# Nine of the sixteen small means of squares of a layer in rounded halves

## The reference, cut to what matters

```python
def rms_norm(x, g):
    xf = x.astype(jnp.float32)
    y = xf * lax.rsqrt(jnp.mean(xf * xf, axis=-1, keepdims=True) + EPS)
    return (y * g.astype(jnp.float32)).astype(x.dtype)
...
def diff_attention(q, k, v, cos, sin, q_g, k_g, lam, lam_init, out_g):
    q = rms_norm(q.reshape(b, s, DA_HEADS, 2, DA_HEAD_DIM), q_g)   # 4 heads, halves of 64
    k = rms_norm(k.reshape(b, s, DA_HEADS, 2, DA_HEAD_DIM), k_g)
    ...  # rotary, two softmaxes, (softmax1 - lam * softmax2) V
    o = rms_norm(o, out_g) * (1.0 - lam_init)
...
def hgrn2_bidirectional(q, z_fwd, z_bwd, inp, gate, lb_fwd, lb_bwd, out_g):
    ...  # gated linear recurrence, forward and backward, 4 heads
    o = rms_norm(o, out_g) * jax.nn.silu(g)
...
for l in range(2):
    proj = rms_norm(x, mix_norm_g[l]) @ w_in[l]                    # 512 x 1024 @ 1024 x 4096
    y_a, y_b = diff_attention(...), hgrn2_bidirectional(...)
    x = x + concat(y_a, y_b) @ w_out[l]
    x = x + conv_glu_ffn(rms_norm(x, ffn_norm_g[l]), ...)          # width 2816
```

## Time and profile before

| | |
|---|---|
| median of 3 runs | 1406.78 us (1406.6 to 1406.83) |
| the profiled execution | 1406.73 us, its span 1404.9 us |
| TensorE busy | 1385.8 us, 99% |
| VectorE busy | 848.9 us, 60% |
| GpSimd busy | 707.9 us, 50% |
| ScalarE busy | 615.2 us, 44% |
| granted TensorE clock | 1.0 throughout |

### The profile page before, as it was taken

One profiled execution on the slowest core, in us unless ns is written; L12 is line 12 of the kernel. 1 busy time (PEld: TensorE's weight loads), 2 busy tenths in 40 slices (PEclk: granted clock), 3 DMA queues, 4 the chain that ended last, 5 costly groups with the idle time before them and its releaser, 6 DMA issues.

```text
span 1404.9 us, 18804 instructions
## 1 busy us (share of the span) xinstructions
PE 1385.8 (99%) x6562; PEld 1118.2 (80%) x6562; DVE 848.9 (60%) x1096; ACT 615.2 (44%) x881; POOL 707.9 (50%) x539
## 2 busy tenths in 40 slices
PE   9999999999999999999998999999999999999999
PEld 6887777877788888888877877778777888888887
DVE  7686797555777676600358758875557766775001
ACT  6352565474444444312444336654744444443111
POOL 2785475337444444444567845652474444444443
PEclk9999999999999999999999999999999999999999
DMA  5222112123233323333222321221122322333333
GB/s 185 76 82 92 46 53 76 46 69 97 80 100 93 103 90 90 105 95 103 90 90 61 90 84 46 71 60 58 61 90 90 105 90 90 99 97 104 90 96 114
DMA packets 37124, 121.31 MB, mean 86 GB/s; under 512 B 4928, under 2 KB 5440, under 8 KB 37056
## 3 DMA queue, kind: packets, MB, share of 16 engines
q1 hardware_dynamic: 36768, 119.84, 27.6%
q10 hardware_dynamic: 288, 0.52, 0.1%
HBM read 114.05 MB, written 2.10 MB: 83 GB/s over the span
## 4 chain that ended last, share of the span: by engine, by line
PE 80%; POOL 6%; issue 6%; DVE 4%; ACT 3%; DMA 0%; POOLq 0%; DVEq 0%; ACTq 0%
PE bank L546 23%; PE bank L548 22%; PE bank L547 22%; PE bank L629 3%; POOL wL L486 2%; PE bank L687 2%; PE bank L705 2%; PE bank L588 2%; POOL rstd L400 1%; POOL wL L480 1%; POOL KK L513 1%; PE bank L696 1%; DVE hL L388 1%; PE bank L660 1%; ACT wH L870 1%
## 5 line engine op out<-in xcount | busy, mean ns | idle before, releaser
L486 POOL TENSOR_TENSOR wL<-raw,wH 128x1024 fp32r<-128x1024 f32 x142 | 342.4, 2411 | 417.5 <-ACT wH L878 356.4
L546 PE MATMUL bank<-hH,wH 128*128 128x512 f32 x1216 | 486.1, 400 | 8.5 <-POOL wL L486 3.5
L548 PE MATMUL bank<-hL,wH 128*128 128x512 f32 x1216 | 474.6, 390 | 0.0
L547 PE MATMUL bank<-hH,wL 128*128 128x512 f32 x1216 | 474.0, 390 | 0.0
L480 POOL TENSOR_TENSOR wL<-raw,wH 128x256 fp32r<-128x256 f32 x268 | 246.8, 951 | 185.0 <-ACT wH L870 185.0
L546 PEld LDWEIGHTS bank<-hH,wH 128*128 128x128 f32 x1216 | 228.3, 188 | 80.5 <-issue 19.2
L548 PEld LDWEIGHTS bank<-hL,wH 128*128 128x128 f32 x1216 | 228.2, 188 | 49.5
L547 PEld LDWEIGHTS bank<-hH,wL 128*128 128x128 f32 x1216 | 228.6, 188 | 44.3 <-issue 0.5
L878 ACT ACTIVATE wH<-raw 128x1024 fp32r<-128x1024 f32 x116 | 122.6, 1057 | 181.1 <-PE bank L548 181.1
L870 ACT ACTIVATE wH<-raw 128x1024 fp32r<-128x1024 f32 x93 | 98.3, 1057 | 141.2 <-PE bank L548 141.0
L546 PE MATMUL bank<-gH,wH 128*128 (+1 forms) x352 | 137.3, 390 | 0.0
(11 more groups left out here) (166 smaller groups left out, 1742.7 us busy)
## 6 DMA issues: line engine op xcount, KB each, us to landing
raw<-wts SPq DMA_DIRECT2D x210, 512.0 KB, 3.5
x<-xT SPq DMA_DIRECT2D x8, 256.0 KB, 5.2
swp<-K SPq DMA_DIRECT2D x32, 64.0 KB, 2.0
swp<-QO SPq DMA_DIRECT2D x32, 64.0 KB, 2.5
outT<-x SPq DMA_DIRECT2D x8, 256.0 KB, 2.0
raw<-wts ACTq DMA_DIRECT2D x2, 256.0 KB, 4.4
raw<-wts SPq DMA_DIRECT2D x2, 256.0 KB, 5.4
W<-pos SPq DMA_DIRECT2D x1, 256.0 KB, 5.8
```

The source lines that it names most:

```text
L486: pool.tensor_tensor(wL[:, s, :], raw[:, s, :], wH[:, s, :].bitcast(F32), ALU.subtract)\
L546: pe.matmul(out, wH[:, s, a:a + P], rhs_h, start=first, stop=False)
L547: pe.matmul(out, wL[:, s, a:a + P], rhs_h, start=False, stop=False)
L548: return pe.matmul(out, wH[:, s, a:a + P], rhs_l, start=False, stop=last)
```

## The change

`PARTED` names nine of the sixteen means: those of slots 13, 14, 18, 25, 26, 27, 30, 31 and 32. For these ScalarE squares the tile twice, once rounded to fp32r into `sqR[:, 0]` and once in fp32 into `sq[:, 1]`. VectorE subtracts the first from the second into `sqR[:, 1]` (`square_low`). TensorE multiplies both fp32r tiles by an fp32r copy of the constants, `meanR`, into the same bank. `sqR` takes the memory of `sq`, so the upper plane is no more free for alternating: all means use plane 1, and each square waits for the mean before it. `meanR` is written once, by ScalarE in slot 12 of the first layer, after the sine.

```diff
+PARTED = [job for s, job in STATS.items() if s < 19 or 24 < s < 33]
...
-        sq = sb("sq", [P, 2, S])
+        sq = sb("sq", [P, 2, S], F32, parts)
+        parts.close()
+        sqR = sb("sqR", [P, 2, S], F32R)
...
+        meanR = sb("meanR", [P, 2 * P], F32R)
...
                     def stat(job):
-                        pe.wait_ge(*squared.at(l, JOB[job] + 1))
+                        if job not in PARTED:
+                            pe.wait_ge(*squared.at(l, JOB[job] + 1))
+                            bank6(("stat", job))
+                            pe.matmul(bank[6][:], cst_at(C_MEAN_H if job in ROPES else C_MEAN_D), sq[:, 1, :],
+                                      start=True, stop=True).then_inc(bank6_full.sem, 1)
+                            return
+                        if l == 0 and JOB[job] == 0:
+                            pe.wait_ge(mean_set, 1)
+                        pe.wait_ge(*part_low.at(l, PARTED.index(job) + 1))
                         bank6(("stat", job))
-                        pe.matmul(bank[6][:], cst_at(C_MEAN_H if job[0] in ("dk", "dq") else C_MEAN_D), sq[:, JOB[job] % 2, :],
-                                  start=True, stop=True).then_inc(bank6_full.sem, 1)
+                        means = meanR[:, P:2 * P] if job in ROPES else meanR[:, 0:P]
+                        pe.matmul(bank[6][:], means, sqR[:, 0, :], start=True, stop=False)
+                        pe.matmul(bank[6][:], means, sqR[:, 1, :], start=False, stop=True).then_inc(bank6_full.sem, 1)
...
                         kind, hd = job
-                        src = sq[:, JOB[job] % 2, :]
+                        j = JOB[job]
+                        if j:
+                            act.wait_ge(*bank6_full.at(l, BANK6[("stat", JOBS[j - 1])] + 1))
...
-                        act.activation(src, of, ACT.Square).then_inc(squared.sem, 1)
+                        if job in PARTED:
+                            act.activation(sqR[:, 0, :], of, ACT.Square)
+                        act.activation(sq[:, 1, :], of, ACT.Square).then_inc(squared.sem, 1)
...
+                                act.activation(meanR[:], cst_at(C_MEAN_D, 2 * P), ACT.Copy).then_inc(mean_set, 1)
...
+                    def square_low(job):
+
+                        dve.wait_ge(*squared.at(l, JOB[job] + 1))
+                        dve.tensor_tensor(sqR[:, 1, :], sq[:, 1, :], sqR[:, 0, :].bitcast(F32), ALU.subtract).then_inc(part_low.sem, 1)
...
                             if lv == CARRY:
                                 states(pair, 0)
+                        if STATS.get(s) in PARTED:
+                            square_low(STATS[s])
                         if step_of(s) is not None:
                             row_max(step_of(s))
```

More of the change, by code:

```diff
@@ L62 @@
          31: ("hgo", 2), 32: ("hgo", 3), 34: ("dao", 3)}
+PARTED = [job for s, job in STATS.items() if s < 19 or 24 < s < 33]
 JOB = {job: j for j, job in enumerate(STATS.values())}
+JOBS = list(JOB)
 OUT_HEADS = [("dao", 0), ("dao", 1), ("dao", 2), ("hgo", 0), ("hgo", 1), ("hgo", 2), ("hgo", 3), ("dao", 3)]
@@ L167, in build @@
     heads = ExitStack()
+    parts = ExitStack()
     ffn = ExitStack()
@@ L265, in build @@
         squared = signal("squared", 16)
+        part_low = signal("part_low", len(PARTED))
+        mean_set = sem("mean_set")
         rstd_ln = signal("rstd_ln", 16)
```

## The result

The changed kernel takes 1412.47 us (median of 6 runs, 1411.71 to 1413.21); before takes 1406.8 beside it (6 runs, 1406.6 to 1407.74). The ratio is 1.0037, with an interval of 1.0026 to 1.0048: slower by 5.7 us between the medians (5.2 by the ratio), and outside the range that was forecast (1404.0 to 1411.9). The profiled execution took 1411.71 us with a span of 1409.9, 4.98 more than the one of before.

What follows compares the result with a forecast made beforehand. TensorE, busy 99% of the span, was taken to bound the kernel, with slot 32's stretch ScalarE's. Layer 0 +1.59 and layer 1 +0.74 gave together +2.3 on 1406.73: 1409.1 us, own range 1407.8 to 1410.6, 8-in-10 range 1404.0 to 1411.9.

Steps and rivals of the forecast that it cites:

- the feed-forward parts: ScalarE's loop of ten rounds per layer after the mixing part; the forecast sum had no term for it.
- Behind it nothing changes: Slot 32, after ScalarE's delayed copy of the gated head: later work keeps its timing, so TensorE's turn starts 3.14 us later.
- The knot: Slot 32: subtraction ahead of maxima and gating delays ScalarE's copy of the gated head, costing 3.14 us per layer.
- The first rival: Slot 32: VectorE's maxima and gating do not hold ScalarE, so the total is 1402.8 to 1403.8 us; chance 10%.
- The gain per mean: TensorE at each changed mean: two fp32r matmuls take 0.45 us in place of 0.86, saving 0.41.
- the five slots: Slots 18, 25, 26, 27 and 30: enough slack to keep every mean's gain, 2.05 us per layer.
- The third rival: At the means: fp32r pairs between fp32 work cost what fp32 did, gains lost, 1413.6 us; chance 5%.
- Slots 13 and 14: Later squares and the subtraction delay the products before the level matmuls: layer 0 +0.5 us (0.2 to 0.9), layer 1 -0.35.
- Slot 14's own gain: Slot 14, both layers: the mean's saving is lost because the projections after it wait for GpSimd's split.
- Slots 26 and 27: VectorE's eviction moves to about 235.1, transposes are due at 235.3: no wait, 0.2 us to spare.
- The rival on the slower side: Slots 26 and 27: VectorE's queue overflows, TensorE waits 1.2 us per layer at transposes, 1411.5 us; chance 22%.
- the place for which I had quoted it: Slots 26 and 27: the shared-port rule was quoted for subtraction and rotary operations waiting on GpSimd splits, giving 1411.5 us.

Runs made afterwards that it cites:

- Experiment 1: The kernel before, with 25 (layer 0) and 24 (layer 1) semaphore increments added on ScalarE that nobody waits for; 1410.09 us beside 1407.62, ratio 1.0017.
- experiment 2: The changed kernel with 7 (layer 0) and 8 (layer 1) more semaphore increments on ScalarE; 1409.49 us, ratio to before 1.0016.
- experiment 5: Only the mean of slot 32 made in two halves, all others in fp32 as before; 1412.99 us beside 1406.86, ratio 1.0043.
- experiment 3: The changed kernel with VectorE's subtraction moved behind the maxima, grow products and gating, all nine means still in halves; 1406.2 us, ratio to before 0.9993.
- experiment 4: The changed kernel with slot 32's mean left in fp32, the other eight in halves; 1404.71 us, ratio to before 0.9981.
- experiment 6: The changed kernel with `meanR` made in slot 6 instead of slot 12 of layer 0; 1411.09 us, ratio to before 1.003.
- experiment 7: Changed kernel with fourteen means in halves (all but slots 32 and 34), subtraction behind the gating, `meanR` made in slot 6; 1401.71 us, ratio to before 0.996.
- experiment 8: Changed kernel with means of slots 13, 18, 19, 22, 23, 25, 26, 27, 30, late subtraction, `meanR` in slot 6, 7 and 8 increments; 1400.67 us, ratio 0.9952.

## Why the prediction was wrong
**Where it failed.** The sum put the feed-forward parts at nothing, without a reason: "Layer 0: +0.5 - 2.05 + 3.14 = +1.59. Layer 1: -0.35 - 2.05 + 3.14 = +0.74" has no term for them, and "Behind it nothing changes" is said of slot 32 alone. The runs put +2.2 there (0.81 + 1.42), through a wait of TensorE for a split, once per turn, which was there before and had no slack. Experiment 1 has it alone (+2.3) and experiment 2 takes it back; so the cause is shown to be instructions added to ScalarE's program ahead of the loop, not anything they do. By what mechanism their number changes the distance is open (last section). With this term the sum would have been 1411.3 (1409.1 + 2.2), 0.4 from the profiled execution; without it the forecast was 2.6 short of the profiled execution and 3.4 of the median.

**The knot.** Right in place, mechanism and size: 3.14 forecast, 3.13 and 3.12 measured, 3.13 alone (experiment 5). That all of it is VectorE's order, but for 0.52 of ScalarE's second square, is shown by experiment 3. The first rival, that the knot is not paid, is refuted.

**The gain per mean.** 0.41 forecast, 0.39 measured in the five slots of both layers: the halves cost 0.47 in place of 0.45. The third rival, a change that does nothing, is refuted by the same number.

**Slots 13 and 14.** The mechanism was right, the size in layer 0 was off: 0.75 for 0.5, within 0.2 to 0.9. The chain itself came as forecast: by the times of the trace with TensorE's 0.10 added, the first square starts at 98.23 (98.22 forecast), so the 0.3 for `meanR` was right; the subtraction starts at 99.40 (99.39) and holds VectorE for 1.20 (1.07), the products take 2.37 (2.52) and end at 102.97 (103.0). That already gives the 0.6, from which the prediction then took 0.1 for a faster second product; it came as that, but the longer subtraction used it up. TensorE starts the level matmuls 0.65 late, and they then take 1.80 to the next projection instead of 1.70. Slot 14's own gain is lost in both layers, as forecast. Layer 1 agrees (-0.33 for -0.35).

**Slots 26 and 27.** The rival on the slower side is refuted: the eviction ends at 235.00, forecast 235.1, and the transposes do not wait. That the measured time lies near this rival's 1411.5 is chance; it has another reason, which no rival had. What the rival drew on did show elsewhere: the eighteen subtractions take 0.68 to 1.38 us, 1.01 in the mean. Six of them run beside no GpSimd operation and take 0.68; each of the other twelve ends 0.54 to 0.55 us after the GpSimd operation that was running as it started (the later one where two overlapped). The one of slot 32 (290.63 to 291.79) is an example: a split runs from 290.50 to 291.24. The rule of the Trainium skill on the shared port (SBUF — State Buffer, section "SBUF: two separate sides") agrees with these twelve ends; it only does not decide the place for which I had quoted it. The price of such a wait is thus what is left of the running operation, here 0.1 to 0.7 us.

**From 1411.7 to 1412.5.** The profiled execution was the fastest of the six; the median lies 0.76 higher. The granted clock of the runs differs a little (0.996 to 1.0), which is the subject of the last section. The prediction had taken before's distance of 0.05 between the two.

## What to carry to other kernels
An instruction that waits for another engine is placed by what is queued behind it: the same subtraction cost 3.1 us ahead of the maxima and 0.5 behind the gating, and moving it in both layers gave 5.2 us, more than the ten means of the five slots gave together (3.9). Where the bounding engine waits once per turn of a loop for a chain without slack, every instruction that a change adds to the program ahead of that loop belongs in the sum as a risk (here -0.6 to +1.4 us per layer), and before the effect of a small change is believed, a control with the same number of empty instructions tells it apart. When a change is spread over many places, take the shift of the bounding engine place by place: it turned one number of +5.0 into terms that could be held against the forecast one by one, and showed that one was missing.

## What the runs showed that was not expected
**The distance from one turn of a loop to the next depends on where its code stands.** The same instructions take 0.538, 0.580 or 0.658 us from the copy to the rounding, each constant over the turns within 0.002 but for the first and the last. Within the turn the trace shows delays of 0.078 us at single instructions: between the branch and the instruction behind it (0.161 or 0.238), at the register operation ahead of the branch (0.02 or 0.098 after the copy), and at the last ones ahead of the rounding. What decides it is open: with 419 instructions ahead of the loop in layer 0 (before), 436 and 443 the distance was 0.580, with 444 (after) 0.658, with 449 and 451 it was 0.538. The Trainium skill (Runtime: NRT & Kernel Launch, section "Instruction fetch mechanics") says that instructions are fetched in blocks, in sequence, and that a taken branch can break this. The trace speaks against such a fetch as the cause here. The packets that carry instructions are listed in the profile's DMA part; in the profile after, between 395 and 600 us, where eight turns are late by the same 0.078, there are seven:
```profile
q8 instruction: 7, 0.11, 0.2%
```
They come 26 to 32 us apart, the turns every 22 us. There are as many in the kernel before, and neither has one there of q14, the other queue that carries instructions. So no packet goes with the delay of a turn, and its cause is not known.

**Short dips of TensorE's clock.** In the profile after, slot 32 of layer 1, in stretches of 1 us (start:end and its length in us; busy us of PE, PEld, DVE, ACT and POOL, with instructions; then the granted clock, DMA share and GB/s):
```profile
995.00:996.00 1.00, 0.20 (x1) 0.23 (x2) 0.91 (x3) 1.00 (x3) 0.00 (x0) 1.00 0.24 94
996.00:997.00 1.00, 1.00 (x5) 0.85 (x5) 0.56 (x1) 1.00 (x4) 0.00 (x0) 0.63 0.08 16
997.00:998.00 1.00, 1.00 (x8) 1.00 (x6) 0.86 (x4) 0.99 (x1) 0.00 (x0) 0.50 0.00 0
...
999.00:1000.00 1.00, 1.00 (x5) 0.83 (x4) 0.90 (x2) 1.00 (x1) 0.00 (x0) 0.67 0.00 0
```
TensorE has waited 2.52 us at the knot, until 995.80; 0.5 us after it starts again the granted clock falls from 1.0 to 0.5 (2.4 to 1.2 GHz) for 3.4 us. Here most of it lies in ScalarE's stretch and costs little: slots 31 and 32 cost 3.12 with this dip and 3.13 in layer 0 without one. The dip of experiment 2 at the start of layer 1 cost about 0.95 net, and of before's 33 runs beside experiments 1 to 4 the 14 at a mean clock of 1.0 took 1406.55 to 1407.24, the 18 at 0.999 took 1407.53 to 1408.43: one dip more or less moves a run by about 1 us, and so a median of before between 1406.8 and 1407.7. Kernels with the idle at the knot are lower oftener (after and experiments 2, 5 and 6: 17 of 29 runs under 0.999) than those without it (before beside experiments 1 to 4, and experiments 1, 3, 4, 7 and 8: 2 of 76). The profiles say the same more closely: in those of the four kernels with the idle, the clock fell once each at one of the two knots, 0.5 to 1.4 us after TensorE had started again from a wait of 2.15 to 2.52 us (layer 0 in experiment 5, layer 1 in the others), and once more at the start of layer 1 in experiment 2; in those of the six kernels without it, nowhere between the first 8 and the last 2 us. So such a wait does not always bring a dip: four of eight did. That the idle causes the dips is argued from this, not shown; no run took the idle away and nothing else.
